# Two experts to one gather, picks and gates in one product, and weight splits moved ahead of the router, in a two-layer hybrid block

## The reference

```python
def moe_swiglu(x, router_w, router_b, w_gate, w_up, w_down):
    logits = (xt @ router_w).astype(jnp.float32) + router_b.astype(jnp.float32)
    top_logit, top_e = lax.top_k(logits, TOP_K)           # 2 of 8 experts
    gate = jax.nn.softmax(top_logit, axis=-1)
    ...                                                   # rows sorted by expert, in blocks
    def block(args):
        xb = x_pad[tok]
        return swiglu(xb, w_gate[e], w_up[e], w_down[e])  # silu(x@g) * (x@u) @ d, width 2816
    y_rows = y_rows * rows_g[:, None]
    out = jnp.zeros((t + 1, d), x.dtype).at[rows_tok].add(y_rows)[:t]
```

## Time and profile before

| | |
|---|---|
| median of the runs | 1584.35 us |
| span of the profiled execution | 1582.1 us |
| TensorE, share busy | 97% (1542.1 us) |
| VectorE | 78% (1236.4 us) |
| ScalarE | 60% (944.3 us) |
| POOL | 2% |
| HBM | 409 MB read, 259 GB/s over the span |
| a weight split on ScalarE, 128x2048 | 1.91 us |
| a weight split on VectorE, 128x2048 | 2.29 us |
| loads from moe_up, issue to landing | 6.7 us |

### The profile page before, as it was taken

One profiled execution on the slowest core, in us unless ns is written; L12 is line 12 of the kernel. 1 busy time (PEld: TensorE's weight loads), 2 busy tenths in 40 slices (PEclk: granted clock), 3 DMA queues, 4 the chain that ended last, 5 costly groups with the idle time before them and its releaser, 6 DMA issues.

```text
span 1582.1 us, 22024 instructions
## 1 busy us (share of the span) xinstructions
PE 1542.1 (97%) x7752; PEld 1293.9 (82%) x7752; DVE 1236.4 (78%) x1217; ACT 944.3 (60%) x872; POOL 27.6 (2%) x65
## 2 busy tenths in 40 slices
PE   6999999999999999999899999999999999999995
PEld 5898888888878898888688888888888888888884
DVE  5679866655456689766898898988889888898885
ACT  5347534644444356533677776777777777777774
POOL 2000000000000000000000000000000000000000
PEclk9999999999999999999999999999999999999997
DMA  8545555555555455546999999999999999999960
GB/s 270 174 153 173 174 166 187 186 187 186 186 186 188 148 187 181 191 144 204 359 364 366 326 367 327 363 365 325 365 328 364 365 324 367 329 362 366 323 242 28
DMA packets 287471, 411.17 MB, mean 260 GB/s; under 512 B 13168, under 2 KB 215968, under 8 KB 287408
## 3 DMA queue, kind: packets, MB, share of 16 engines
q1 hardware_dynamic: 284720, 401.73, 75.6%
q0 software_dynamic: 2688, 8.61, 1.7%
HBM read 409.24 MB, written 1.05 MB: 259 GB/s over the span
## 4 chain that ended last, share of the span: by engine, by line
PE 92%; DVE 4%; ACT 1%; issue 1%; DMA 1%; SPq 0%; DVEq 0%; ACTq 0%
PE ps L991 30%; PE ps L614 20%; PE ps L1000 14%; PE ps L882 8%; PE ps L604 4%; PE ps L896 4%; PE ps L593 3%; PE ps L940 2%; DVE w_lo L1789 1%; PE ps L969 1%; PE ps L950 1%; DVE w_lo L1394 1%; ACT w_hi L1064 1%; DMA raw_m<-w_in_dram 1%; PE ps L572 0%
## 5 line engine op out<-in xcount | busy, mean ns | idle before, releaser
L1789 DVE TENSOR_TENSOR w_lo<-late,w_hi 128x2048 fp32r<-128x2048 f32 x192 | 438.4, 2290 | 42.1 <-ACT w_hi L1284 42.1
L1284 ACT CAST w_hi<-late 128x2048 fp32r<-128x2048 f32 x192 | 367.5, 1914 | 43.3 <-PE ps L991 43.3
L1394 DVE TENSOR_TENSOR w_lo<-raw_m,w_hi 128x2048 fp32r<-128x2048 f32 x117 | 267.4, 2290 | 141.3 <-ACT w_hi L1064 141.0
L1064 ACT CAST w_hi<-raw_m 128x2048 fp32r<-128x2048 f32 x117 | 222.1, 1906 | 143.5 <-PE ps L614 67.4
L991 PE MATMUL ps<-w_hi,hT_hi 128*128 128x512 f32 x704 | 281.7, 400 | 2.9 <-DVE w_lo L1789 2.9
L991 PE MATMUL ps<-w_hi,hT_lo 128*128 128x512 f32 x704 | 274.9, 390 | 0.0
L991 PE MATMUL ps<-w_lo,hT_hi 128*128 128x512 f32 x704 | 274.6, 390 | 0.0
L614 PE MATMUL ps<-w_hi,hT_hi 128*128 128x512 f32 x480 | 191.3, 398 | 1.9 <-DVE w_lo L1394 1.0
L614 PE MATMUL ps<-w_hi,hT_lo 128*128 128x512 f32 x480 | 188.2, 392 | 0.0
L614 PE MATMUL ps<-w_lo,hT_hi 128*128 128x512 f32 x480 | 188.2, 392 | 0.0
L1789 DVE TENSOR_TENSOR w_lo<-raw_m,w_hi 128x2048 fp32r<-128x2048 f32 x72 | 164.9, 2292 | 26.0 <-ACT w_hi L1284 26.0
(11 more groups left out here) (335 smaller groups left out, 2169.8 us busy)
## 6 DMA issues: line engine op xcount, KB each, us to landing
late<-moe_down_dram SPq DMA_DIRECT2D x144, 512.0 KB, 5.7
raw_m<-w_in_dram SPq DMA_DIRECT2D x128, 512.0 KB, 4.6
late<-moe_gate_dram SPq DMA_DIRECT2D x120, 512.0 KB, 5.3
late<-moe_up_dram SPq DMA_DIRECT2D x120, 512.0 KB, 6.7
raw_m<-moe_gate_dram SPq DMA_DIRECT2D x56, 512.0 KB, 5.3
raw_m<-moe_up_dram SPq DMA_DIRECT2D x56, 512.0 KB, 6.7
raw_m<-moe_down_dram SPq DMA_DIRECT2D x32, 512.0 KB, 5.1
raw_m<-ffn_gate_dram SPq DMA_DIRECT2D x22, 512.0 KB, 4.0
```

The costliest lines, as they stand in the source:

```text
L1064: copy(w_hi[:, g % RS, :], slot_raw(g, False)).then_inc(hi_ready, 1)
L1284: copy(w_hi[:, j % RS, :], slot_raw(j, True)).then_inc(hi_ready, 1)
L1394: tt(w_lo[:, g % RS, :], slot_raw(g, False), w_hi[:, g % RS, :], ALU.subtract)\
L1789: tt(w_lo[:, j % RS, :], slot_raw(j, True), w_hi[:, j % RS, :], ALU.subtract).then_inc(lo_ready, 1)
```

## The change

- **Pairs.** The loops run over four pairs. `sel` holds the picks of both experts of a pair side by side, and one gather gives both: columns 0 to 127 of `hT` for the first, 128 to 255 for the second. It stands ahead of the last chunk of the pair's second expert; at the end of the first expert there is none.
- **Rounded halves.** The rows are kept as `xn_hi` and `xn_lo` (f32r), and each is multiplied with the picks by itself: eight fills of (0, 1, 6, 7, 3, 2, 6, 7) in that order, hi and lo in turn. ScalarE copies the even ones to `hT_hi`, VectorE the odd ones to `hT_lo`.
- **Rows.** POOL multiplies `xt` with the norm gain as soon as each piece of it is complete (`xg`); ScalarE makes `xn_hi`, VectorE `xn_lo`.
- **Picks and gates.** One product for each token tile with `idg`, an identity with two gate columns (rounded gate and remainder) ahead of it, gives the transposed picks and the gates.
- **First splits.** Chunk 0 of the experts is split before the w_o result is taken through the router (on VectorE between the two halves of w_o), chunk 1 stays where it was.
- Some tiles move: `ysb_hi` and `ysb_lo` lie over the masks, `xn_lo` over `tmp`, `idg` over `bias`. SyncE's stream is unchanged.

```diff
@@ POOL
+            pool.dma_start(ffn_g, ffn_norm_g[L - 1].partition_broadcast(P)).then_inc(fg_in, 16)
+            pool.wait_ge(fg_in, 32)
+            for h, name in enumerate(("wo", "wo'")):
+                for t in range(NT):
+                    b, k = FILL[L - 1, name, t]
+                    pool.wait_ge(drained[b], k + 1)
+                    c = slice(h * W, (h + 1) * W)
+                    nc.gpsimd.tensor_tensor(xg[:, t, c], xt[:, t, c], ffn_g[:, c], ALU.mult).then_inc(xg_ready, 1)
+            pool.wait_ge(xg_ready, 2 * NT)
             pool.dma_start(fin_g, final_g.partition_broadcast(P)).then_inc(fg_in, 16)
@@ TensorE
-            def gather(banks, waits):
+            def gather(fill):
+                for q in range(8):
+                    b, k = fill(q)
+                    pe.wait_ge(drained[b], k)
+                    src = (xn_hi, xn_lo)[q % 2]
+                    for kk in range(2):
+                        k = 2 * (q // 2) + kk
                         for t in range(NT):
-                            ins = mm(ps[:, banks[i], kk * P:(kk + 1) * P], xn[:, t, k * P:(k + 1) * P], sel[:, t, :],
+                            ins = mm(ps[:, b, kk * 2 * P:(kk + 1) * 2 * P], src[:, t, k * P:(k + 1) * P], sel_pair(t),
                                      start=(t == 0), stop=(t == NT - 1))
...
-                with pe.Fori(0, E) as e:
+                with pe.Fori(0, EP) as p:
+                    for x in range(2):
...
-                        if n == FFC - 1:
-                            pe.wait_ge(sel_ready, pas * (E + 1) + 2 + e)
-                            gather([f[0] for f in fb], [f[1] for f in fb])
+                            if x == 1 and n == FFC - 1:
+                                pe.wait_ge(sel_ready, pas * (E + 1) + 3 + 2 * p)
+                                gather(lambda q: moe_fill(pas, p, 1, "gather", q))
...
-                            for t in range(NT):
-                                nc.tensor.transpose(ps[:, b, t * P:(t + 1) * P], sel[:, t, :], ident[:, :])
-                            for t in range(NT):
-                                ins = mm(ps[:, b, T:T + 1], sel[:, t, :], gcur[:, t:t + 1], start=(t == 0),
-                                         stop=(t == NT - 1))
+                                for t in range(NT):
+                                    ins = mm(ps[:, b, t * (P + 2):(t + 1) * (P + 2)], sel(t, x), idg[:, t, :],
+                                             start=True, stop=True)
@@ ScalarE
                 ahead(l, "wo", 1)
+                if l == L - 1:
+                    ahead(l, "wo'", 1)
+                    split_moe(0, 0, 0)
                 for i in range(2):
                     hi_of(l, "fnorm", i, hT_hi, C_FG)
...
+            act.wait_ge(rstd_ready, 2 * L)
+            act.wait_ge(xg_ready, 2 * NT)
+            for t in range(NT):
+                A(xn_hi[:, t, :], xg[:, t, :], ACT.Copy, scale=rstds[:, 2 * L - 1, t:t + 1]).then_inc(xh_ready, 1)
             act.wait_ge(router_d2, 1)
             A(g12[:, :, 0:1], g12[:, :, 0:1], ACT.Exp).then_inc(router_e, 1)
-            for j in range(2):
-                split_moe(0, 0, j)
+            split_moe(0, 0, 1)
+            def gather_hi(fill):
+                for q in range(0, 8, 2):
+                    b, k = fill(q)
+                    act.wait_ge(full[b], k + 1)
+                    copy(hT_hi[:, q:q + 2, :], ps[:, b, :].rearrange("p (m n) -> p m n", m=2)).then_inc(drained[b], 1)
...
+                        if m == 2 * FFC - 1:
+                            gather_hi(lambda q: moe_fill(pas, p, 1, "gather", q))
+                        if m + 2 < 2 * FFC or not last:
+                            split_moe(pas, p, m + 2)
@@ VectorE
                     if h:
                         ahead(l, "wo'", 1)
+                    elif l == L - 1:
+                        ahead(l, "wo'", 1)
+                        split_moe(0, 0, 0)
                     for i in range(2 * h, 2 * h + 2):
                         lo_of(l, "fnorm", i, hT_hi, hT_lo, C_FG)
...
+            def rows_lo(t):
+                dve.wait_ge(xh_ready, t + 1)
+                stt(xn_lo[:, t, :], xg[:, t, :], r[:, t:t + 1], xn_hi[:, t, :], ALU.mult, ALU.subtract)\
+                    .then_inc(xl_ready, 1)
...
+            def gate_columns(col, nth):
+                g = gmat[:, :, col]
+                V.tensor_copy(idg[:, :, 0:1], g).then_inc(gate_hi, 1)
+                dve.wait_ge(gate_hi, nth)
+                return tt(idg[:, :, 1:2], g, idg[:, :, 0:1], ALU.subtract)
+            def gather_lo(fill):
+                for q in range(1, 8, 2):
+                    b, k = fill(q)
+                    dve.wait_ge(full[b], k + 1)
+                    V.tensor_copy(hT_lo[:, q - 1:q + 1, :], ps[:, b, :].rearrange("p (m n) -> p m n", m=2))\
+                        .then_inc(drained[b], 1)
...
                             b = moe_full("selT")
-                            V.tensor_copy(gslot, ps[:, b, T:T + 1])
-                            V.tensor_copy(selT, ps[:, b, 0:T].rearrange("p (t n) -> p t n", t=NT))\
-                                .then_inc(drained[b], 1)
-                            V.tensor_copy(gcur.unsqueeze(2), gmat[:, :, bass.ds(e + (pas * E + 1), 1)])
-                            select(bass.ds(e + (pas * E + 1), 1))
+                            v = ps[:, b, 0:NT * (P + 2)].rearrange("p (t n) -> p t n", t=NT)
+                            V.tensor_reduce(gslot, v[:, :, 0:2], mybir.AxisListType.XY, ALU.add)
+                            V.tensor_copy(selT(x), v[:, :, 2:P + 2]).then_inc(drained[b], 1)
+                            if x:
+                                gate_columns(bass.ds(2 * p + (pas * E + 2), 1), p * 2 + (pas * (E + 1) + 3))
+                                select(lambda y: bass.ds(2 * p + (pas * E + 2 + y), 1), True)
+                            else:
+                                gate_columns(bass.ds(2 * p + (pas * E + 1), 1), p * 2 + (pas * (E + 1) + 2)).then_inc(sel_ready, 1)
```

More of the change, by code:

```diff
@@ L115, in program, with pfills @@
     fills(1, "rank", (0,))
-    EXPERT, nexp = {}, [0] * 8
-    def efills(tag, banks):
+    EP = E // 2
+    PAIR, npair = {}, [0] * 8
+    def pfills(x, tag, banks):
         for i, b in enumerate(banks):
[L121 to L132, removed]
+            PAIR[x, tag, i] = (b, npair[b])
+            npair[b] += 1
+    for x_ in range(2):
+        for i in range(NF):
+            pfills(x_, f"gu{i}", ((i + x_) % 2,))
+            pfills(x_, f"hT{i}", (2,))
+        pfills(x_, "selT", (3,))
+        pfills(x_, "acc", (4, 5))
+        pfills(x_, "sc0", (6, 7))
+        pfills(x_, "sc1", (6, 7))
+    GBANKS = (0, 1, 6, 7, 3, 2, 6, 7)
+    pfills(1, "gather", GBANKS)
+    PRO = {b: GBANKS.count(b) for b in GBANKS}
+    EPI = {6: 2, 7: 2}
     PASS_FILL = [[nfill[b] for b in range(8)]]
-    PASS_FILL.append([PASS_FILL[0][b] + E * nexp[b] + PRO.get(b, 0) + EPI.get(b, 0) for b in range(8)])
+    PASS_FILL.append([PASS_FILL[0][b] + EP * npair[b] + PRO.get(b, 0) + EPI.get(b, 0) for b in range(8)])
     USED, n_used = [], 0
@@ L156, in program @@
     MOE_USED0 = n_used
[L157 to L166, removed]
+    PUSED, PU = [], 0
+    for x_ in range(2):
+        for kind, i, c in FF:
+            if kind == "gu" and c == 1:
+                PUSED.append(("bank", (x_, f"gu{i}", 0)))
+            elif kind == "dn" and i == NF - 1:
+                PUSED.append(("bank", (x_, "acc", 1)))
+            else:
+                PU += 1
+                PUSED.append(("w", PU))
     ctx = ExitStack()
@@ L180, in program @@
         xt = sb("xt", [P, NT, D])
+        xn_at = here()
         xn = sb("xn", [P, NT, D])
@@ L190, in program @@
         cols = sb("cols", [P, L, NCOL])
+        ones = sb("ones", [P, 2])
+        st = sb("st", [P, 128])
+        cnt_i = sb("cnt_i", [P, 1], i32)
+        masks_at = here()
         cmask = sb("cmask", [P, 384], bf16)
@@ L1844, in gates_of_picks, with select @@
                 settle()
-            def select(col):
-                for t in range(NT):
-                    ins = ts(sel[:, t, :], iota, pos[:, t, col], None, ALU.is_equal)
-                ins.then_inc(sel_ready, 1)
-            def gather_lo(banks, waits, nh):
-                for i in range(2):
-                    dve.wait_ge(full[banks[i]], waits[i])
-                    dve.wait_ge(hi_part, nh + i + 1)
-                    r = slice(4 * i, 4 * i + 4)
-                    tt(hT_lo[:, r, 0:P], ps[:, banks[i], :].rearrange("p (m n) -> p m n", m=4), hT_hi[:, r, 0:P],
-                       ALU.subtract).then_inc(drained[banks[i]], 1)
+            def select(col, last):
+                for x in range(2):
+                    for t in range(NT):
+                        ins = ts(sel(t, x), iota, pos[:, t, col(x)], None, ALU.is_equal)
+                if last:
+                    ins.then_inc(sel_ready, 1)
```

350 lines of the change are left out of this document (184 added, 166 removed).

## The result

Measured against runs of the kernel before on the same chip, the change is slower: 1603.62 us (1603.08 to 1605.29) against 1584.51, ratio 1.0122, 95% interval 1.011 to 1.0133. The forecast was 1580.0. The profiled execution spans 1601.8 us, 19.7 more than before's 1582.1.

A forecast was written before the change was run, and what follows sets the result against it. TensorE bounds, with 92% of the chain of waits. -5.3 + 1.7 - 2.7 + 0.6 + 0.6 + 0.7 = -4.4 us gives a span of 1577.7, a run median of 1580.0; range 1575.5 to 1585.0.

The forecast's parts named there:

- Gathers: Expert stage: nine gathers become five, one per pair; four of 3.50 us go, four become 0.36 longer.
- Inside a pair: Four boundaries between a pair's experts: last down chunk starts 1.33 us earlier without the gather; -5.3 us (-3.6 to -14.0).
- between pairs: Four boundaries where the new gather waits for its own evacuation: +0.42 us each, +1.7 us (+1.2 to +4.0).
- The gap of 2.1 us: Sign of being right: TensorE idles about 2.1 us between transposes and last down chunk, until VectorE's remainder.
- Picks and gates: Two products of 0.12 us replace 0.58 us on TensorE: -0.34 for each expert, -2.7 us (-1.0 to -2.7).
- The late split at the second expert of a pair: VectorE's extra selections and copies make a split late by about 0.2 us, three times: +0.6 us (0 to +1.5).
- Start: Start of the experts: early first split, gained rows, later first gather and third chunk; together +0.6 us (0 to +2.5).
- Code: TensorE's doubled loop: branch costs 2.8 to 3.5 us if not held, mostly hidden; +0.7 us for three (0 to +10).
- Rival (c): Backward branches of TensorE or VectorE lose 2.8 to 3.3 us each in the open: +9, 1588.5 us; chance 0.09.
- VectorE's branches: Half of Rival (c): VectorE branches only with the last remainder, losing 2.8 to 3.3 us each; whole rival's chance 0.09.
- Rival (d): Inside a pair, the new 2.1 us wait lowers TensorE's clock: 2 us lost, four times +8, 1588 us; chance 0.05.
- The 1.27 us wait: Start of the experts: TensorE's wait until 774.72 in before, with the clock at full, cited against Rival (d).

The follow-up runs named there:

- e9: Kernel of e5 with the first expert's first weight tile split behind the router's chain again, as in before: 1575.52 us, 0.9947 of before.
- e8: Kernel before with TensorE's eight passes over the experts written out in place of its loop: 1584.23 us, 1.0004 of before.
- e2: Kernel before with two experts in TensorE's loop body and 4 passes, same matmuls in the same order: 1601.49 us, 1.0104 of before.
- e3: Kernel after with VectorE forming the last hidden tile's low half ahead of the next split inside a pair: 1592.11 us, 1.0051 of before.
- e4: Kernel after with a prefetch hint for TensorE's backward branch at the top of every pass: 1603.66 us, 1.012 of before.
- e7: Kernel of e3 with the branch's prefetch hint set four weight slots ahead of the loop's end: 1593.97 us, 1.0055 of before.
- e11: Kernel before with 56 satisfied waits ahead of each weight slot, TensorE's loop body 1942 instructions: 1810.79 us, one run.
- e1: Kernel after with TensorE's four passes over the pairs written out in place of its loop: 1583.8 us, 0.9994 of before.
- e5: Kernel after with the edits of e1 and e3 together: 1575.89 us, 0.9951 of before.
- e10: Kernel before with 42 satisfied waits ahead of each weight slot, TensorE's loop body 1711 instructions: 1759.67 us, one run.
- e6: Kernel before with 28 satisfied waits ahead of each weight slot, TensorE's loop body 1480 instructions: 1646.69 us, 1.0402 of before.

## Why the prediction was wrong, step by step

- **Gathers.** Inside a pair 1.26 us came off, forecast 1.33; between pairs +0.44, forecast +0.42. The gap of 2.1 us was there, ended by VectorE's remainder. Mechanism and size right.
- **Picks and gates.** -0.32 for each expert, forecast -0.34. The late split at the second expert of a pair cost one wait of 0.3 us, not three of 0.2.
- **Start.** No run shows that the new first gather takes as long as the old, from which the prediction has its end near 768.2: it held TensorE from 762.41 to 768.73, 6.32 us, in place of 5.44 (762.27 to 767.71), and the clock was at 0.50 until 767.8, in before until 766.1. In all the start was +0.8, forecast +0.6; e9 puts the early split in it at nothing. That these agree is not shown by one execution each: in e8 and e2, which leave before's start as it is, the third chunk starts at 774.04 and 776.07, where before has 774.72.
- **Code, the step that failed.** It said "so it can lose 3.3 us there without being seen", and +0.7 for three branches. The lead was real: the branch is taken at 964.24 and the last matmul ahead of it starts at 967.10. The price was wrong. I took 2.76 us, the idle time at the jump at the end of the program. That row showed what TensorE lost there, not how long the branch took, which in the kernel before was 3.41 us:

```profile
L1033 PEldq COMPARE_BRANCH  x1: 3411/3411/3411, 1567.2 to 1567.2; - x1
```

  Even by this row a branch would have shown only 0.1 us past the lead of 3.3. Among the experts the branches that miss take 5.8 to 6.7 us (kernel after, e2, e3, e4, e7). From the branch at 964.24 to the next matmul it is 6.92 us; the last chunk covers 3.09 of it (until 967.33), and 3.83 are seen. Three of them: 11.8 us in place of 0.7. Why they take twice as long as the jump at the end stays open. The DMAs are nearly idle at that jump (share 0.03 from 1586 to 1594 us of the kernel after), but their load alone doesn't explain it: the share was 0.92, 0.88 and 0.80 during the three branches of the kernel after, and in e11, at 0.94 to 1.02, the branches took 3.8 to 4.5 us, no more than its jump at the end with a share of 0.05 (4.67). What differs is how soon the code packet starts: 3.7 to 3.9 us behind the branch in the kernel after, 1.2 to 1.9 in e11, 1.1 at the jump at the end of the kernel after. From its landing to the end of the branch it is 1.3 to 1.6 us in all of these.
- **Rival (c)** named this mechanism and its decision point (1.5 us a branch) and had 0.09; its price, 2.8 to 3.3 each, was under the 3.9 measured, and it left out what the clock does behind such a gap, 8.5 us more. Its other half, VectorE's branches, did not come: they take 50 to 72 ns in the kernel after, as before. The granted clock fell behind 13 of 15 branches of the five kernels with a long body and unpadded stages (kernel after, e2, e3, e4, e7).
- **Rival (d)** had 0.05 and came true beside (c), 5.1 us: it fell behind 7 of 12 waits of 2.1 us (kernel after, e1, e4) and none of 12 waits of 1.0 us (e3, e5, e7). The 1.27 us wait with which I argued against it lies on the harmless side; it said nothing of 2.1.
- I treated (c) and (d) as alternatives with a chance each. They come from different places (e1 takes away one, e3 the other) and add up, and with them the forecast's own terms still hold: -5.0 + 1.8 - 2.6 + 0.3 + 0.8 = -4.7, then 11.8 + 8.5 + 5.1, is +20.7. The profiled difference is 19.7. The tail accounts for 1.3 us of the other sign: before has the low clock for 19.3 us at its end, the kernel after for 16.7, and half of it is lost; that leaves +19.4.

## What to carry to other kernels

Count the instructions of a hardware loop's body on the engine that bounds the kernel before making it longer: up to 1480 the backward branch took 0.2 us here, at 1711 and more it took 3.8 to 6.7 us, and code written out straight cost nothing measurable (e1, e8). Price an idle gap on TensorE with the clock behind it: gaps at the branches, near 4 us, cost 1.7 to 3.4 us more in 13 of 15 cases, waits of 2.1 us 1.7 more in 7 of 12, those of 1 us nothing in 12, so moving one small operation ahead of a big one (e3) was worth twice the wait it took away. Where two rivals don't exclude each other, price them together too. Price a branch by its own row and not by the idle time it left somewhere else, and give it a wide range: even that row (3.41 us) was short of the 6.3 us that followed.

## What the runs showed of the hardware that was not expected

- A loop body over the bound loses all of its code, not the part that is over: 1711 instructions, some nine packets a pass; 1480, none.
- A missed branch has no fixed price: 3.3 to 6.7 us in these kernels. The last code packet ahead of its end starts 0.9 to 4.1 us behind its start and lands 1.3 to 1.6 us ahead of its end; in e10's loop, where two packets come at once, it lands 1.5 to 2.4 us ahead.
- The prefetch hint cost 38 ns and changed nothing, at either place.
- Padding of satisfied waits isn't free: 3696 instructions of it (8 experts x 462) cost 62 us, 17 ns each, in a stream that was 97% busy with matmuls.
- In six of the executions (e1, e6, e7, e9, e10, e11) the clock also fell near 231 us, and in e1, e7 and e9 near 692 us, in stretches that the edits don't touch; the profiled execution of the kernel before didn't show it, but three of the six (e6, e10, e11) are that kernel with padding later on. It moves a single profiled span by up to 5 us (e9: 3.4 and 6.8 us at 0.50, half of it lost), so differences of a few us are read from medians.
